# First MLP matmul with the weights stationary and 256 tokens streaming, in a two-block transformer kernel on one core

## What is computed

```python
h2 = rmsnorm(x, g_mlp[l])                                    # (256, 2048)
u = jax.nn.relu(jnp.einsum('bsd,df->bsf', h2, w_up[l]))      # w_up: (2048, 8192)
x = x + jnp.einsum('bsf,fd->bsd', u * u, w_down[l])          # w_down: (8192, 2048)
```

## Time and profile before

| | |
|---|---|
| Runs before | 2182.67 us median of 3 (2181.71 to 2185.63) |
| Profiled execution, first to last instruction | 2180.3 us (it has no time of its own beside this span) |
| PE busy | 2038.3 us, 93% of the span |
| PE weight loads busy | 1667.9 us, 76% |
| DVE busy | 1270.9 us, 58% |
| ACT busy | 1020.5 us, 47% |
| Granted TensorE clock, mean | 0.971 |

### The profile page before, as it was taken

The page is one execution under the profiler, slowest core; times in us unless marked ns, Lnnn a source line. Parts: engine busy times, 40 slices in busy tenths (PEclk is TensorE's granted clock), DMA queues, the critical chain, the costliest instruction groups (busy, mean ns, idle before and its releaser), DMA issues.

```text
span 2180.3 us, 24124 instructions
## 1 busy us (share of the span) xinstructions
PE 2038.3 (93%) x9141; PEld 1667.9 (76%) x9141; DVE 1270.9 (58%) x1191; ACT 1020.5 (47%) x1346; POOL 23.0 (1%) x25
## 2 busy tenths in 40 slices
PE   3499469999999999998999999999999999999997
PEld 1378358888888888887778778788888888888886
DVE  7978986555655454456546556654544454454454
ACT  3043245444444544444556654554445444544543
POOL 0000010000000000000000000000000000000000
PEclk9699669999999999999999999999999999999999
DMA  9999977666675555555454454455555555555552
GB/s 400 420 348 358 333 251 252 236 234 242 232 248 174 191 186 194 183 193 174 136 174 159 152 172 143 166 174 193 183 194 187 188 192 192 178 189 194 190 186 103
DMA packets 193757, 463.03 MB, mean 212 GB/s; under 512 B 7401, under 2 KB 7849, under 8 KB 180753
## 3 DMA queue, kind: packets, MB, share of 16 engines
q1 hardware_dynamic: 191808, 455.11, 60.6%
q0 software_dynamic: 848, 3.70, 0.5%
q10 hardware_dynamic: 1024, 3.20, 0.4%
HBM read 459.87 MB, written 2.10 MB: 212 GB/s over the span
## 4 chain that ended last, share of the span: by engine, by line
PE 86%; DVE 9%; ACT 2%; issue 1%; DMA 1%; ACTq 0%; DVEq 0%; SPq 0%
PE ps L419 27%; PE ps L421 27%; PE ps L420 27%; DVE scr L1107 6%; PE ps L455 2%; DVE w_low L1095 1%; DMA raw<-in_w_mod 1%; ACT w_high L779 1%; PE ps L555 0%; PE ps L557 0%; DVE h_both L1186 0%; PE ps L429 0%; PE ps L442 0%; PE ps L449 0%; ACT L993 0%
## 5 line engine op out<-in xcount | busy, mean ns | idle before, releaser
L1095 DVE TENSOR_TENSOR w_low<-raw,w_high 128x1024 fp32r<-128x1024 f32 x672 | 820.8, 1225 | 813.0 <-ACT w_high L779 812.8
L779 ACT ACTIVATE w_high<-raw 128x1024 fp32r<-128x1024 f32 x672 | 708.6, 1059 | 886.5 <-PE ps L421 870.1
L419 PE MATMUL ps<-w_high,h_both 128*128 128x512 f32 x1536 | 610.1, 397 | 8.5 <-DVE w_low L1095 7.6
L421 PE MATMUL ps<-w_high,h_both 128*128 128x512 f32 x1536 | 600.8, 391 | 0.0
L420 PE MATMUL ps<-w_low,h_both 128*128 128x512 f32 x1536 | 600.1, 391 | 0.0
L419 PE MATMUL ps<-w_high,u_high 128*128 128x512 f32 x1152 | 451.0, 392 | 0.3 <-DVE u_low L1489 0.3
L421 PE MATMUL ps<-w_high,u_low 128*128 128x512 f32 x1152 | 448.6, 389 | 0.0
L420 PE MATMUL ps<-w_low,u_high 128*128 128x512 f32 x1152 | 448.3, 389 | 0.0
L419 PEld LDWEIGHTS ps<-w_high,h_both 128*128 128x128 f32 x1536 | 289.8, 189 | 68.6 <-DVE w_low L1095 5.7
L421 PEld LDWEIGHTS ps<-w_high,h_both 128*128 128x128 f32 x1536 | 289.4, 188 | 62.0
L420 PEld LDWEIGHTS ps<-w_low,h_both 128*128 128x128 f32 x1536 | 290.0, 189 | 58.2 <-issue 0.5
(11 more groups left out here) (171 smaller groups left out, 819.9 us busy)
## 6 DMA issues: line engine op xcount, KB each, us to landing
raw<-in_w_mod SPq DMA_DIRECT2D x96, 1024.0 KB, 7.0
raw<-in_w_mlp_in SPq DMA_DIRECT2D x64, 1024.0 KB, 5.7
raw<-in_w_mlp_out SPq DMA_DIRECT2D x64, 1024.0 KB, 5.0
raw<-in_w_up SPq DMA_DIRECT2D x64, 1024.0 KB, 5.5
raw<-in_w_down SPq DMA_DIRECT2D x64, 1024.0 KB, 5.0
raw<-in_w_in SPq DMA_DIRECT2D x48, 1024.0 KB, 5.1
raw<-in_fnet_w SPq DMA_DIRECT2D x16, 1024.0 KB, 6.2
raw<-in_w_out SPq DMA_DIRECT2D x16, 1024.0 KB, 5.0
```

Of the source, the lines that this page charges most:

```text
L419: eng.matmul(dst, ah, wh, start=(k == 0), stop=False)
L421: last = eng.matmul(dst, al, wh, start=False, stop=(k == KT - 1))
L779: eng.activation(w_high[:, h % LEAD, :], raw[:, slot, (h % 2) * 2 * CW:(h % 2 + 1) * 2 * CW], ACT.Copy).then_inc(high_ready, 1)
L1095: eng.tensor_tensor(w_low[:, h % LEAD, :], raw[:, slot, piece], w_high[:, h % LEAD, :].bitcast(f32), ALU.subtract).then_inc(raw_used if h ...
```

## The change

Only the first matmul of both MLPs changes. `half_up` takes the 128x128 blocks of the weights as the stationary operand and streams all 256 tokens of `h_high` or `h_low`. A half is four blocks b by two slices k by three matmuls, 24 matmuls of 256 columns in the place of 12 of 512. The result has the hidden columns on the partitions and the tokens along the bank, as the second matmul wants them. The turns, their semaphore `t_posed` and the wait for `mod_cols` that the first of them carried are gone. ACT copies `hidden` from SBUF to `u_high` in one operation of 1024 columns right behind the square, and DVE makes `u_low` from `hidden` in one operation. With tokens along the free dimension the norm's scale can no longer be put on with the relu: the second block leaves it out there, and since relu and square of a positive multiple give that multiple squared, DVE multiplies by `rstd_2` = rstd squared when it adds the second matmul's result to x (`add_scaled_step`, two operations of 512 columns in the place of one of 1024).

```diff
+            def half_up(n, hh):
+                slot = t.c["half"] % LEAD
...
+                for b in range(4):
+                    dst = lin(n)[:, b // 2, (b % 2) * SEQ:(b % 2 + 1) * SEQ]
+                    for kk in range(2):
+                        k = 2 * hh + kk
+                        wh = w_high[:, slot, kk * CW + b * P:kk * CW + (b + 1) * P]
+                        wl = w_low[:, slot, kk * CW + b * P:kk * CW + (b + 1) * P]
+                        eng.matmul(dst, wh, h_high[:, k, :], start=(k == 0 and b % 2 == 0), stop=False,
+                                   skip_group_check=True)
+                        eng.matmul(dst, wh, h_low[:, k, :], start=False, stop=False, skip_group_check=True)
+                        last = eng.matmul(dst, wl, h_high[:, k, :], start=False, stop=(k == KT - 1),
+                                          skip_group_check=True)
+                last.then_inc(half_used, 1)
...
-            def turn_hidden(tt, mods_read):
-                if tt == 0:
-                    eng.wait_ge(up_ready, t.at("up", 0))
-                if t.c["t"] % (2 * NC):
-                    eng.wait_ge(t_low, t.at("t", 0))
-                elif mods_read:
-                    eng.wait_ge(mod_cols, mods_read)
-                turn(side(0), hidden[:, tt, :]).then_inc(t_posed, 1)
-                t.add("t")
...
-                        step(c, c, h_high, h_low, h_ready if c == 0 else lambda hh: None)
+                        for hh in range(HALVES):
+                            if c == 0:
+                                h_ready(hh)
+                            half_up(c, hh)
+                            mod_passed(4 * c + hh // 2)
...
-                    if 1 <= c <= NC and hh in (1, 3):
-                        tt = hh // 2
-                        t.add("t")
-                        eng.wait_ge(t_posed, t.at("t", 0))
-                        eng.activation(u_high[:, 4 * (c - 1):4 * c, tt * P:(tt + 1) * P],
-                                       side(0).rearrange("p (b n) -> p b n", b=4), ACT.Copy).then_inc(t_high, 1)
...
-                            if scaled:
-                                for tt in range(TT):
-                                    last = eng.activation(relu[:, tt, :], lin(c)[:, tt, :], ACT.Relu,
-                                                          scale=rstd[:, tt:tt + 1])
-                                last.then_inc(up_taken, 1)
-                            else:
-                                eng.activation(relu, lin(c), ACT.Relu).then_inc(up_taken, 1)
+                            eng.activation(relu, lin(c), ACT.Relu).then_inc(up_taken, 1)
                             eng.wait_ge(up_taken, t.at("up", 0))
+                            if t.q is not None or t.c["t"]:
+                                eng.wait_ge(t_low, t.at("t", 0))
+                            t.add("t")
                             eng.activation(hidden, relu, ACT.Square).then_inc(up_ready, 1)
+                            eng.wait_ge(up_ready, t.at("t", 0))
+                            eng.activation(u_high[:, 4 * c:4 * c + 4, :], hidden.rearrange("p t (b n) -> p (t b) n", b=2),
+                                           ACT.Copy).then_inc(t_high, 1)
...
+            def add_scaled_step(target, n, c):
+                eng.wait_ge(half_used, t.at("done", 0))
+                for tt in range(TT):
+                    piece = target[:, tt, c * CW:(c + 1) * CW]
+                    last = eng.scalar_tensor_tensor(out=piece, in0=lin(n)[:, tt, :], scalar=rstd_2[:, tt:tt + 1],
+                                                    in1=piece, op0=ALU.mult, op1=ALU.add)
+                last.then_inc(summed, 1)
```

More of the change, by code:

```diff
@@ L423, in half @@
                 t.add("half")
+            def half_up(n, hh):
+                slot = t.c["half"] % LEAD
+                if t.c["half"] % 2 == 0:
+                    t.add("chunk")
+                    eng.wait_ge(low_first, t.at("chunk", 0))
+                else:
+                    t.add("raw")
+                    eng.wait_ge(raw_used, t.at("raw", 0))
+                for b in range(4):
[10 more added lines that the diff above has]
+                last.then_inc(half_used, 1)
+                t.add("half")
             def sum_partitions_to_columns(v, place):
@@ L477, in h_ready, with mlp, mod_passed @@
                     eng.wait_ge(n_low, t.c["stage"] + 2 + hh)
[L479 to L499 removed]
+            def mlp(start, stop, mods=()):
+                def mod_passed(chunk):
+                    if t.c["half"] % 2 == 0 and chunk - 2 in mods:
+                        t.add("raw")
+                with t.loop(eng, start, stop, half=64, chunk=32, raw=32 + len(mods), summed=NC, up=NC, t=NC):
                     for c in range(NC):
@@ L511, in mlp @@
                             eng.wait_ge(summed, t.at("summed", -1))
-                        def hidden_ready(hh):
+                        for hh in range(HALVES):
                             if c == 0 and hh % 2 == 0:
-                                eng.wait_ge(t_low, t.at("t", hh + 2 - 2 * NC) if hh < 6 else t.at("t", 0))
-                        step(NC + c, c, u_high, u_low, hidden_ready)
+                                t.add("t")
+                                eng.wait_ge(t_low, t.at("t", 0))
+                            half(c, hh, u_high, u_low)
+                            mod_passed(4 * (NC + c) + hh // 2)
                         t.add("summed")
@@ L1206, in gain, with mlp_body @@
                    .then_inc(final_gained, 1)
-            def mlp_body(target, q=0, mods=(), ahead=True, after=None, last=None):
+            def mlp_body(target, q=0, mods=(), ahead=True, after=None, last=None, step=add_step):
                 for y in range(64):
@@ L1535, in _ @@
             invert()
-            with t.loop(eng, 0, QUARTERS - 1, low=64, raw=32, t=2 * NC, done=64, squared=TT * NC, summed=NC) as q:
-                mlp_body(xs)
+            link(eng.tensor_tensor(rstd_2[:, :], rstd[:, :], rstd[:, :], ALU.mult))
+            with t.loop(eng, 0, QUARTERS - 1, low=64, raw=32, t=NC, done=64, squared=TT * NC, summed=NC) as q:
+                mlp_body(xs, step=add_scaled_step)
             eng.wait_ge(grow_in, 48)
-            mlp_body(xs, ahead=False, after=gain, last=lambda: gain(NC - 1))
+            mlp_body(xs, ahead=False, after=gain, last=lambda: gain(NC - 1), step=add_scaled_step)
             mean_square()
```

44 lines of the change are left out of this document (18 added, 26 removed).

## The result

| | median us | lowest to highest | runs |
|---|---|---|---|
| before | 2182.89 | 2181.71 to 2185.63 | 4 |
| after | 2195.32 | 2194.81 to 2196.16 | 4 |

The changed kernel is slower by 12.4 us; the ratio is 1.0054, with a 95% interval of 1.0041 to 1.0066. In a second comparison, made later, it took 2192.77 us against 2183.84, ratio 1.0046 (1.0032 to 1.0059). So the loss is 9 to 12 us. The prediction of 2154.5 us was wrong in sign.

The account below looks back on a forecast made before the run. PE's own list was taken as the bound. Terms -31.1 + 1.8 + 0.8 + 0.3 = -28.2 us took the median from 2182.67 to 2154.5 us, with a range of 2147 to 2180.

Parts of the forecast that it names:

- turns: Between the MLP matmuls on PE: 64 groups of four transposes removed, 0.486 us each, -31.1 us.
- s: Step from start to start of a 256-column matmul in the first MLP matmul, taken as 113.6 ns.
- stream: First MLP matmul on PE: 6144 matmuls of 256 columns replace 3072 of 512, +1.8 us.
- borders: At 16 borders between the two matmul shapes, uneven starts of the first 10 matmuls, 5 ns each: +0.8 us.
- ACT, DVE: Splitting, copy and square work at step ends in the MLPs: stays hidden behind PE, adds nothing.
- end: Behind the kernel's last matmul, DVE's scaled add as two 512-column operations instead of one: +0.3 us.
- the 4.2 us of cover: At step ends in the MLPs: time left between DVE finishing the split and PE needing it, 4.2 us.
- rival 5: ACT's burst at step ends makes PE wait because the cover fails; 2183 us, no difference; chance 0.03.
- The break-even: First MLP matmul: the 256-column step, 118.3 ns, below which the changed kernel is faster.
- Rival 3: First MLP matmul: fixed 13.3 ns per matmul, step 120.0 ns, net +11, about 2193 us; chance 0.12.
- Rival 2: First MLP matmul: starts never become even, step 116.0 ns, net about -14 us, 2169 us; chance 0.24.
- Rival 4: First MLP matmul: every matmul waits for its whole load of 189 ns, +465, about 2617 us; chance 0.04.

Follow-up runs that it names:

- run 3: Kernel before plus 14 stretches of 32 matmuls behind PE's last, varying width and load; 256 columns: 119.7 ns with full load, 113.8, 113.1, 115.6 with 64, 32, 8.
- run 6: Kernel before plus stretches of 48 fp32r matmuls at its end, varying load and width; 256 columns: 119.8 ns with load of 128, 113.3 with 64.
- run 1: Changed kernel with its first matmul put back to tokens stationary, 512 columns, output fed on untransposed; 2152.61 us against 2184.55, ratio 0.985.
- run 2: Kernel before, transposes kept, each 512-column matmul of the first MLP matmul cut into two of 256; 2224.27 us against 2184.55, ratio 1.0178.
- run 4: Changed kernel with matmuls sharing w_high paired into one of 512 columns, w_low by h_high left at 256, alternating; 2185.43 us against 2184.55, ratio 1.0004.
- run 7: Changed kernel loading only 64 of 128 columns of each weight block in the first matmul; 2164.07 us against 2183.84 for the kernel before, ratio 0.9919.
- run 5: Paired wide-and-narrow kernel, reordered so each half does eight 512-column matmuls, then eight of 256; 2182.67 us against 2183.84 for the kernel before, ratio 0.999.
- run 11: Changed kernel with paired matmuls grouped over two halves, sixteen of 512 columns, then sixteen of 256; 2180.57 us against 2185.08 for the kernel before, ratio 0.9982.
- run 10: Changed kernel loading 112 of 128 columns of each weight block in the first matmul; 2173.45 us against 2185.08 for the kernel before, ratio 0.9955.

## Why the prediction was wrong, step by step

**The step that failed** is the one on the load: "So a load needs some 111.7 ns if nothing else holds it, 1.6 ns less than the stream of 113.3: it stays hidden, but barely". Both numbers were right, and runs 3 and 6 measured them apart (111.0 to 111.3 and 113.3). The conclusion wasn't: together they take 120.0 ns, not the larger of the two. So s was 120.0 instead of 113.6, and the stream costs 6144 x 120.0 - 696.2 = +41.1 us instead of +1.8. That is 39 us more, the size of the whole error, 37 to 41 us.

**The forecast against the runs, term by term**

| term | predicted | measured | from |
|---|---|---|---|
| turns | -31.1 | -31.9, the end's +0.2 in it | run 1 |
| stream | +1.8 | +41.1 by the step, +39.7 by the time | profile after, run 2 |
| borders | +0.8 | +0.7, 8 x (92.25 - 768 x 0.120) | profile after |
| ACT, DVE | 0 | 0, no new wait of PE | profile after |
| end | +0.3 | +0.2, counted with the turns | profile after |
| sum | -28.2 | +9.9 | time: +12.4, again +8.9 |

The borders came to the predicted size, but not by uneven starts alone: in seven of the eight stages the first narrow matmul takes 0.2 us or more to the next, and the others 120 ns.

**What was right.** PE's own list decides, the turns are worth 0.5 us each, and the 4.2 us of cover held: the new copy on ACT takes 1.061 us and the new `u_low` 1.218, as the sum had them, and no wait came of it (rival 5 had no effect). The break-even, s = 118.3, fits as well: the measured s is above it, and the kernel is slower.

**The rivals.** Rival 3 forecast 120.0 ns and 2193 us, and both came in. Its mechanism did not: 13.3 ns don't go with every matmul, since 256 columns with a small load take 113 ns (run 3). That it hit the number is luck: 106.7 + 13.3 happens to be what a full load and a 256-column stream take together. Both arguments on it, the mean pair of 348 for it and the pair of 340 against it, came from loads of 8 columns, and rows with such loads can't tell what a full load does. Rival 2 had its truth elsewhere: alternating widths can be slower than their parts (run 4), but the changed kernel has only one width in its first matmul and runs evenly. Rival 4 is refuted: a load is on record with 193 ns and steps of 120. The Trainium skill (Perfetto Trace Analysis, "Identifying the Most-Contended Engine") takes the busy share of LDWEIGHTS, beside the useful flops, as a measure of how close TensorE is to its limit. In the first-matmul stages that row is full, 90.0 of 90.0 us from 2004 to 2094; but it is as full in run 7 at steps of 113.4 (85.0 of 85.0 us from 1971 to 2056), so here it doesn't tell the two paces apart. Another sentence of the skill is borne out in kind: TensorE: Matmul & The Clock Gate, "Back-to-back issue gap", says that in a stream of loads and matmuls the spacing is set by both. The trace agrees on that, though not on the section's figure of about 131 ns at 512 columns, where this kernel shows 226.6 in fp32r.

**The range.** I had named 118 to 120 as the upper bound of s and left what lies above 118 to rival 3, with a chance of 0.12. No row of before had a full load beside a stream of 256 columns in fp32r, so nothing in it spoke for 113.6 against 120 but the two separate numbers, 1.6 ns apart. With one nanosecond worth 6 us, that is a margin too thin to put 0.54 on.

**What stays open.** Why a full load and a 256-column stream need 6.7 ns more than either, and why shorter loads fall now into 113.3, now into 116 to 120. The runs exclude a fixed cost per matmul as the reason, the orientation and the choice of PSUM bank; they show no cause. For the pace of the smaller loads, and for that of the alternating pairs in run 4, I found no condition; a stage keeps the pace that it has from its start. What the pause in runs 4, 5 and 11 waits for is open as well.

## What to carry to other kernels

Cutting matmuls from 512 to 256 columns adds no columns, but it isn't free when each brings its own full load: here each narrow one took 6.7 ns more than half of a wide one, and together that was more than the transposes cost that the change saved. When two resources of an engine come within a few ns of each other, don't price the pair at the larger of the two; look for a row with both, and if there is none, run one stretch of a few dozen such matmuls before the kernel is rewritten. If a saving needs narrow matmuls, keep a shared stationary's products together as one wide matmul, and group wide and narrow ones instead of alternating them. And look at the trace of every version for new pauses at its borders before its time is put down to the steps alone.

## What the runs showed of the hardware that was not expected

- The steps of fp32r matmuls with a full load don't follow one line in the width: 240 columns 112.0 ns, 248 113.4, 252 116.7, 256 120.0, 264 120.1, 288 131.7, 320 146.6, 384 174.1, 448 202.5, 512 226.6.
- A full load alone sets a step of 111 ns at 128 and 192 columns; half a load with 128 columns gives 60.0.
- Loads of 96 to 127 columns beside 256 streamed ones took between 113.5 and 120.0 ns, and the one of 112 columns 113.5 in one run and 117.8 in another. In the kernel, stages of one execution with identical instructions ran at 113.4 and at 120 (run 7), or at 113.4 and 117.8 (run 10), and kept that pace for 768 matmuls.
- The extra 6.7 ns showed at the upper level of the clock only: in the first stage of the changed kernel, where the granted clock is 0.50 behind a wait (311 to 316 us), the same full loads and 256-column streams start 213.3 ns apart, which is 256 columns at 1.2 GHz with nothing added.
- A change of width costs the matmuls behind it: 230 ns for each of eight wide ones behind eight narrow ones. An alternating pair takes 353.3 ns in some stages and 346.7 in others.
